# Hyena long convolutions: the spectrum products move from two engines to VectorE alone

## The reference, cut to what matters

```
z      = first gate input                      # 512 channels x 512 tokens
for o in 0, 1:
    K  = spectrum of the learned filter o      # two-sided, computed earlier
    z  = inverse_transform(transform(z) * K) + filt_bias[o] * z
    z  = z * gate[o]
```

## Time and profile before

| | us |
|---|---|
| median of 3 runs | 2830.53 |
| lowest and highest of them | 2829.56, 2836.32 |
| the profiled execution's own time | 2835.54 |
| its span, first to last instruction | 2833.4 |
| busy TensorE (matmuls) | 2466.3 |
| busy VectorE | 1266.7 |
| busy ScalarE | 593.0 |
| busy GpSimd | 192.1 |

### The profile page before, as it was taken

The page is one execution under the profiler, slowest core; times in us unless marked ns, Lnnn a source line. Parts: engine busy times, 40 slices in busy tenths (PEclk is TensorE's granted clock), DMA queues, the critical chain, the costliest instruction groups (busy, mean ns, idle before and its releaser), DMA issues. The chain is left out here.

```text
span 2833.4 us, 42510 instructions
## 1 busy us (share of the span) xinstructions
PE 2466.3 (87%) x18560; PEld 1514.8 (53%) x18560; DVE 1266.7 (45%) x2094; ACT 593.0 (21%) x861; POOL 192.1 (7%) x136
## 2 busy tenths in 40 slices
PE   8977499978999999899756989898989789989887
PEld 6874499956545554487324744343437474434343
DVE  6776766656323322477676531122127742112113
ACT  4343311123111111253401311010113341101001
POOL 0000000013000000010142210000000030000000
PEclk9987699988999999999778989999999899999999
DMA  6560132154999999532010769999973156999996
GB/s 223 183 210 12 53 108 86 56 189 154 418 416 418 416 416 405 230 115 81 21 45 0 296 253 427 428 426 428 427 294 84 40 230 285 427 427 427 428 427 255
DMA packets 121890, 727.04 MB, mean 257 GB/s; under 512 B 12038, under 2 KB 65542, under 8 KB 84679
## 3 DMA queue, kind: packets, MB, share of 16 engines
q1 hardware_dynamic: 92200, 693.82, 60.5%
q10 hardware_dynamic: 29536, 30.93, 3.3%
HBM read 722.63 MB, written 2.10 MB: 256 GB/s over the span
## 5 line engine op out<-in xcount | busy, mean ns | idle before, releaser
L2080 PE MATMUL ps<-s_ring,s_c_XG 128*64 128x512 f32 x2016 | 471.7, 617 | 76.8 <-DMA s_ring<-in_exp_w 62.5
L2080 PEld LDWEIGHTS ps<-s_ring,s_c_XG 128*64 128x64 f32 x2016 | 158.7, 142 | 374.1 <-issue 340.3
L2194 DVE TENSOR_TENSOR s_c_hid<-ps,s_c_sil 128x512 f32<-128x512 f32 x32 | 34.4, 1074 | 508.2 <-PE ps L2080 508.2
L2121 PE MATMUL ps<-s_ring,s_c_hidT 128*64 128x512 f32 x1024 | 223.4, 594 | 0.0
L2080 PE MATMUL ps<-s_ring,s_m_XG 128*64 128x512 f32 x1024 | 222.9, 593 | 0.0
L2080 PEld LDWEIGHTS ps<-s_ring,s_m_XG 128*64 128x64 f32 x1024 | 72.8, 137 | 142.7 <-issue 141.6
L2121 PEld LDWEIGHTS ps<-s_ring,s_c_hidT 128*64 128x64 f32 x1024 | 72.5, 137 | 137.0 <-issue 136.8
L371 PE MATMUL ps<-s_src_part,s_w_hi_at 128*128 128x512 f32 x384 | 123.8, 404 | 1.1 <-DVE s_src_part L1589 1.0
L2206 DVE SCALAR_TENSOR_TENSOR s_c_Y_lo<-ps,s_c_w_slot,s_c_Y_hi 128x512 fp32r<-128x512 f32 x32 | 22.6, 747 | 211.5 <-ACT s_c_Y_hi L2163 211.5
L2121 PE MATMUL ps<-s_ring,s_m_hidT 128*64 128x512 f32 x512 | 113.4, 595 | 0.0
L371 PE MATMUL ps<-s_h_part,s_w_hi 128*128 128x512 f32 x336 | 106.3, 398 | 2.8 <-DVE s_w_lo L349 2.8
(11 more groups left out here) (636 smaller groups left out, 4456.6 us busy)
## 6 DMA issues: line engine op xcount, KB each, us to landing
s_ring<-in_exp_w SPq DMA_DIRECT2D x190, 2048.0 KB, 17.3
s_ring<-in_moe_w_gate SPq DMA_DIRECT2D x32, 2048.0 KB, 12.2
s_ring<-in_moe_w_up SPq DMA_DIRECT2D x32, 2048.0 KB, 14.8
s_ring<-in_moe_w_down SPq DMA_DIRECT2D x32, 2048.0 KB, 12.1
s_mod_w_at<-in_vectors SPq DMA_DIRECT2D x64, 512.0 KB, 4.2
s_mod_w<-in_vectors SPq DMA_DIRECT2D x48, 512.0 KB, 4.5
s_w_raw<-in_w_in ACTq DMA_DIRECT2D x13, 1024.0 KB, 8.4
s_w_raw_at<-in_w_in ACTq DMA_DIRECT2D x8, 1024.0 KB, 5.0
```

The costliest lines, as they stand in the source:

```text
L2080: last = nc.tensor.matmul(ps[x * SLOTS:(x + 1) * SLOTS, bank + fh, :], XG[:, k, c0:c0 + SLOTS], columns(w[x], at), start=(k == 0), stop=(k ...
L2121: last = nc.tensor.matmul(ps[rows, DOWN + half, :], hidT[:, f, rows], columns(w[x], at), start=(f == 0), stop=(f == nj - 1))
L2194: nc.vector.tensor_tensor(hid_out[:, fh * per:(fh + 1) * per, :], ps[:, UP + fh, :].rearrange("s (p j) -> s p j", j=nj), sil[:, fh * 512:( ...
```

## The change

GpSimd has no part in the stage any more. Its products are joined to those of VectorE: one instruction handles blocks f and HF + f together, as an access pattern of two runs of 512 elements on each partition (128x1024). The folds too take both f in one instruction. TensorE waits for the folds alone. The strips in the code would divide the channels, but per is CT, so that there is one strip with all 512 channels, and the loop over strips[1:] is empty.

Instructions of one convolution before: on VectorE 8 for the spectra, 12 for products and sums, 8 folds; on GpSimd 12 for products and sums. Afterwards: on VectorE 8 for the spectra (unchanged), 12 for products and sums of double size, 4 folds of double size; on GpSimd none.

```diff
-                m0, a0, v0, e0, p0 = mm_done.n, act_evac.n, dve_out.n, dve_evac.n, pool_out.n
+                m0, a0, v0, e0 = mm_done.n, act_evac.n, dve_out.n, dve_evac.n
+                per = CT
...
                         pe.wait_ge(dve_evac.sem, e0 + 2 * HF)
-                        pe.wait_ge(dve_out.sem, v0 + HF)
-                        pe.wait_ge(pool_out.sem, p0 + 2 * HF)
                         for c in range(CT):
+                            if c % per == 0:
+                                pe.wait_ge(dve_out.sem, v0 + c // per + 1)
...
-                            act.wait_ge(dve_out.sem, v0 + HF)
+                            act.wait_ge(dve_out.sem, v0 + CT // per)
...
-                    def product(eng, f):
-                        eng.tensor_tensor(Y[:, 0, f, :], U[:, 0, f, :], Kc[:, f, o, :], ALU.mult)
-                        eng.tensor_tensor(t1[:, f, 0, :], U[:, 1, f, :], Ks[:, f, o, :], ALU.mult)
-                        eng.tensor_tensor(Y[:, 1, f, :], U[:, 0, f, :], Ks[:, f, o, :], ALU.mult)
-                        return eng.tensor_tensor(t1[:, f, 1, :], U[:, 1, f, :], Kc[:, f, o, :], ALU.mult)
-                    def collect(eng, f):
-                        eng.tensor_tensor(Y[:, 0, f, :], Y[:, 0, f, :], t1[:, f, 0, :], ALU.subtract)
-                        return eng.tensor_tensor(Y[:, 1, f, :], Y[:, 1, f, :], t1[:, f, 1, :], ALU.add)
-                    @block.gpsimd
-                    def _(pool):
-                        for f in range(HF):
-                            pool.wait_ge(dve_evac.sem, e0 + 2 * f + 2)
-                            product(nc.gpsimd, HF + f).then_inc(*pool_out.up())
-                            pool.wait_ge(pool_out.sem, p0 + 2 * f + 1)
-                            collect(nc.gpsimd, HF + f).then_inc(*pool_out.up())
...
-                            vlink(product(V, f))
-                            vlink(collect(V, f))
+                        def product(f, cols):
+                            at = slice(f, None, HF)
+                            u0, u1, kc, ks = U[:, 0, at, cols], U[:, 1, at, cols], Kc[:, at, o, cols], Ks[:, at, o, cols]
+                            y0, y1, p0, p1 = Y[:, 0, at, cols], Y[:, 1, at, cols], t1[:, at, 0, cols], t1[:, at, 1, cols]
+                            V.tensor_tensor(y0, u0, kc, ALU.mult)
+                            V.tensor_tensor(p0, u1, ks, ALU.mult)
+                            V.tensor_tensor(y1, u0, ks, ALU.mult)
+                            vlink(V.tensor_tensor(p1, u1, kc, ALU.mult))
+                            V.tensor_tensor(y0, y0, p0, ALU.subtract)
+                            vlink(V.tensor_tensor(y1, y1, p1, ALU.add))
+                        def fold(cols):
+                            low, high = slice(0, HF), slice(HF, KT)
+                            V.tensor_tensor(B[:, 0, 0, :, cols], Y[:, 0, low, cols], Y[:, 0, high, cols], ALU.add)
+                            V.tensor_tensor(B[:, 0, 1, :, cols], Y[:, 1, low, cols], Y[:, 1, high, cols], ALU.subtract)
+                            V.tensor_tensor(B[:, 1, 0, :, cols], Y[:, 0, low, cols], Y[:, 0, high, cols], ALU.subtract)
+                            V.tensor_tensor(B[:, 1, 1, :, cols], Y[:, 1, low, cols], Y[:, 1, high, cols], ALU.add).then_inc(*dve_out.up())
+                        strips = [slice(n * per * P, (n + 1) * per * P) for n in range(CT // per)]
                         for f in range(HF):
-                            dve.wait_ge(pool_out.sem, p0 + 2 * f + 2)
-                            V.tensor_tensor(B[:, 0, 0, f, :], Y[:, 0, f, :], Y[:, 0, HF + f, :], ALU.add)
...
+                            whole(f)
+                            product(f, strips[0])
+                        fold(strips[0])
+                        for cols in strips[1:]:
+                            for f in range(HF):
+                                product(f, cols)
+                            fold(cols)
```

More of the change, by code:

```diff
@@ L2946, in _, with whole @@
                         V = nc.vector
-                        for f in range(HF):
+                        def whole(f):
                             for q in range(2):
@@ L2952, in _ @@
                             dve.wait_ge(dve_evac.sem, e0 + 2 * f + 2)
-                            vlink(product(V, f))
-                            vlink(collect(V, f))
-                        for f in range(HF):
-                            dve.wait_ge(pool_out.sem, p0 + 2 * f + 2)
-                            V.tensor_tensor(B[:, 0, 0, f, :], Y[:, 0, f, :], Y[:, 0, HF + f, :], ALU.add)
-                            V.tensor_tensor(B[:, 0, 1, f, :], Y[:, 1, f, :], Y[:, 1, HF + f, :], ALU.subtract)
-                            V.tensor_tensor(B[:, 1, 0, f, :], Y[:, 0, f, :], Y[:, 0, HF + f, :], ALU.subtract)
-                            V.tensor_tensor(B[:, 1, 1, f, :], Y[:, 1, f, :], Y[:, 1, HF + f, :], ALU.add).then_inc(*dve_out.up())
+                        def product(f, cols):
[8 more added lines that the diff above has]
+                            vlink(V.tensor_tensor(y1, y1, p1, ALU.add))
```

## The result

| | before | after |
|---|---|---|
| median, us (18 runs each) | 2831.4 | 2817.18 |
| lowest and highest, us | 2823.41, 2840.61 | 2810.39, 2830.62 |
| span of the profiled execution, us | 2833.4 | 2815.0 |

The ratio is 0.995, with a 95% interval of 0.9938 to 0.9961: 14.2 us less, between 11.0 and 17.5. Forecast were 2820.0 and 10.5 us less. The time is in the range, the direction right; the saving is larger than the sum of the steps, and the interval just leaves that sum out.

What follows compares the result with a forecast made beforehand. The bound was taken as each convolution's chain through VectorE's products and folds: 14.12 + 2.52 + 4.90 = 21.54 us instead of 26.79, twice 5.25, so 10.5 us off the 2830.53 median: 2820.0 us, range 2814 to 2827.5.

Steps and rivals of the forecast that it cites:

- The chain: Each convolution: TensorE's spectra, VectorE's products and folds, TensorE's inverse transform; 26.79 us from first product to inverse transform.
- GpSimd as the cause of 1.75 us: VectorE products beside GpSimd: both engines hold each other up, costing each product 1.06 us more than alone.
- The products: VectorE, each product as six double-size instructions: 7.06 us instead of 9.08, 4.04 us less for two.
- The pattern of two runs: Two-block operands on VectorE: no charge, 1.14 us per step; rival with 1.36 us, 2827.0 in all, chance 0.07.
- The folds: VectorE folds through TensorE's release, four double-size instructions: 4.90 us instead of 6.11, 1.21 us less.
- The spectra of f = 1: Between the two products: not late, 1.5 us of slack, four instructions keep their 2.52 us.
- What comes behind: Inverse transform, weights' split, bias and gate, next block's loads: all start earlier by the same amount, nothing given back.
- The gain drowns: Rival: run spread and TensorE restarts in the two convolutions give back 4.8 us, 2824.8 in all; chance 0.12.
- Slow for a reason of its own: Rival: long VectorE products not GpSimd's doing, 3.5 us per double-size instruction, 2866 in all; chance 0.03.
- TensorE's clock: Restart after the idle wait before the inverse transform: cost unchanged, ends 2.4 us gained or lost per convolution.
- The price of a restart: TensorE's first matmuls after idling, at lowered clock: 18 take 5.8 us instead of 3.4, costing 2.4 us.
- the prediction's estimate: GpSimd's work on VectorE at twice its speed: 1.23 us per merged instruction instead of 1.14, leaving 7.6 us saved.

Runs made afterwards that it cites:

- slack: Changed kernel with 5.2 us of extra VectorE work, results unread, in front of each convolution's folds: 2830.22 us, ratio 0.9993.
- moved_only: Changed kernel with every two-block instruction issued as two of 128x512, so GpSimd's work moves but nothing is merged: 2823.62 us, ratio 0.997.
- pool_busy: Changed kernel with GpSimd doing its 12 old instructions per convolution into an unread buffer, the folds waiting for it: 2848.6 us, ratio 1.0056.
- warm: Changed kernel with 36 extra matmuls on TensorE, results unused, in each idle stretch before the inverse transform: 2845.31 us, ratio 1.0048.
- fold_only: Kernel before with only the eight folds merged into four of double size, products still on both engines: 2833.53 us, ratio 1.0008.
- after_again: Changed kernel measured once more without any edit, with a second trace: 2818.86 us, ratio 0.9958.
- warm18: Changed kernel with 18 extra matmuls on TensorE, results unused, in each idle stretch before the inverse transform: 2820.92 us, ratio 0.9966.
- strips4: Changed kernel with per = 1, four strips of 128 channels: 2815.75 us, ratio 0.9939.
- strips2_order: Changed kernel with two strips of 256 channels and the weights' split behind the first two groups' bias and gate: 2806.51 us, ratio 0.9928.
- strips2: Changed kernel with per = 2, two strips of 256 channels, the second beside TensorE's work on the first: 2811.6 us, ratio 0.9932.

## Why the prediction was right, and where its sum was short

- **The chain** (fold on VectorE releases TensorE) was right: lengthening VectorE's stage by 5.1 us in slack brought 13.15 of the 13.36 us back in the trace.
- **GpSimd as the cause of 1.75 us** was right, shown from both sides by moved_only (0.68 us without it) and pool_busy (2.2 us with it, at double size).
- **The products**: 7.06 us forecast, 7.06 measured. The pattern of two runs costs nothing here (1.22 us, the duration of the earlier trace rows). The rival that it does is out.
- **The folds**: 4.90 us forecast, 4.78 measured; the release took 0.15 us (1473.97 + 1.22 to 1475.34), not 0.26.
- **The spectra of f = 1**: no wait, 2.52 us, as forecast.
- **What comes behind**: nothing given back in these traces. "The gain drowns" did not happen.
- **Slow for a reason of its own**: refuted by the result and by moved_only.
- **TensorE's clock** is the term that was mis-sized. I set its change to zero, with 2.4 us either way per convolution. The price of a restart was right: with the clock kept at full in warm, 2.4 and 2.0 us of the stretches of before are gone. Its change was not: it is 2.6 us gained in all, 1.13 behind the two restarts, and 1.5 in the transposes between the convolutions, a place that the working did not look at. Both traces of the changed kernel have it, and none of those with a longer stage (before, fold_only, slack, moved_only, pool_busy). The prediction gave a gain through the clock a chance of 0.03 and a loss through it most of the 0.12 of "drowned"; that the clock shortened the time and did not lengthen it was luck, and the 10.5 us alone lie just outside the first interval.

The sum of the measured parts, with it, is 13.4 us, inside the intervals of both comparisons (11.0 to 17.5 us, and 8.2 to 15.6 us in after_again); the sum without it is inside the second only. What stays open is what sets the place of the clock's switches: no run here varied it by itself, and it is not known in how many of the executions without a trace the 2.6 us are gained. And warm18 shows that removing one slow stretch can bring up another.

By the prediction's estimate from what the Trainium skill states on elementwise work (GPSIMD Engine Reference, Key points: VectorE about twice as fast), 7.6 us would have been saved. Instruction for instruction the runs agree with that page: 0.60 us a step in moved_only against GpSimd's 1.268 us, a factor of 2.1. For the merged form the row of the kernel, 0.54 us for the second 512 elements, was the better guide.

## What to carry to other kernels

Where VectorE's instructions with two SBUF inputs take two to three times their length just while GpSimd runs, the helper costs about what it holds: compare the step alone (0.60 us) with the step beside it (1.67 us) before splitting work by busy shares. Here each GpSimd instruction spared VectorE one of 0.60 us and held it up for 1.07 us. Once an engine's stage is on the path, a start on part of its output can be worth more than larger instructions: in the traces two strips gave 9.4 us on top, four only 1.6, and merging the instructions 5.2, of which 2.2 its own. And a change in a stage's length can move the places where TensorE's clock is low, for better or worse, so look at the short TensorE stretches behind it too.

## What was not expected of the hardware

The granted clock's switches lie at nearly the same distance from the first product in most of the traces, though not in all. Behind the half spectra TensorE is idle from 4.9 us after the first product on. The clock falls from 1.00 to 0.50 between 7.4 and 7.7 us after the first product in before, fold_only, slack, pool_busy, strips4, strips2_order and both traces of the changed kernel. In moved_only and strips2 it falls 10.3 us after it. strips2 and strips2_order run the same instructions up to there; their windows from 7.8 to 10.2 us after the first product, strips2 first, differ in nothing but the clock:

```profile
1464.80:1467.20 2.40, 0.00 (x0) 0.00 (x0) 2.37 (x5) 0.00 (x0) 0.00 (x0) 1.00 0.00 0
1464.90:1467.30 2.40, 0.00 (x0) 0.00 (x0) 2.37 (x5) 0.00 (x0) 0.00 (x0) 0.50 0.00 0
```

So two traces of one kernel that agree don't show that all of its executions do, and whether the slow transposes of moved_only (3.65 us) come from its stage of 22.5 us or from this other place of the switches isn't known.

In both traces of the changed kernel the transposes between the convolutions run at full clock (2.16 and 2.15 us), in before and fold_only mostly at the low one (3.65 and 3.64 us). A stretch of extra matmuls that kept the clock at full (2.4 GHz) through the idle time gained 1.6 us per convolution and lost 2.7 of these 3.2 us in the transposes and half spectra between the two.
